# Two-block transformer kernel: the norms between the blocks and the z gate in one block, turned tile by tile

## The chip, the cores and the metric

The kernel runs on one core of a Trainium2 chip. The time is device microseconds of that core; three runs of the kernel before took 3314.9, 3316.67 and 3316.89 us, median 3316.67.

## The reference, cut to what matters

The program computes two layers one after the other. The first has windowed and latent attention and a mixture of 16 experts; the second has a gated delta rule, banded attention and a gated feed-forward layer. All is float32 on 1024 positions of width 1024. The change lies where the first hands over to the second:

```python
def first_block(...):
        ...
        x = x + g_f * ec_moe(h2, w_router[l], w_gate[l], w_up[l], w_down[l])
        ...
    return rmsnorm(x, norm_final)

def second_block(x, norm_mix_w, w_in, ...):
        h = rmsnorm_2(x, norm_mix_w[l])
        proj = h @ w_in[l]
        qa, ka, va, za, ba, aa, qb, kb, vb, ga, gb = jnp.split(proj, IN_SPLITS, axis=-1)
        ...
        oa = (rmsnorm_2(oa, gdn_norm_w[l]) * jax.nn.silu(za)).astype(x.dtype).reshape(b_, t_, VAL_A)
```

So between the experts and the rest stand two norms in a row (weights norm_final and norm_mix), the turn of h so that features lie on partitions (hT), the product z = h @ w_z (1024x512) with Silu and the weight gdn_norm, and the narrow product for ba and aa.

## The kernel before, in words

The 1024 positions are 8 tiles of 128 (NT = 8), the width is 8 slices of 128 (KD = 8). Each stage is a block: five programs, one for each engine, with hand-written semaphores; a block ends when all its engines have arrived. PSUM is one tensor `banks` of 8 banks of 512 floats a partition. A float32 product stands in the trace as two TensorE instructions (passes), so a z tile (8 products of 128x512) is 16 passes; a transpose is one.

`experts` (L1254) runs 16 experts. For each, TensorE does gate_up (products into banks 2 and 3), turn_x (eight transposes of the next expert's rows, evicted in 128x128 pieces by ScalarE at L1352 and VectorE at L1376), down and turn_h. SP loads the weights three experts ahead into three sets of buffers. The last scatter into expert_sums ends the stage.

`between_blocks` (L1402) takes the tiles of x. SP issues the 8 loads of x, then 17 small constants (L1417, norm_mix the eleventh of them), w_z, w_ba, the first two feature weights, and then each x_rows store when its tile is scaled. VectorE's loop does, per step, `first` of tile t (x times norm_final, L1469), `second` of tile t-1 (a reciprocal, x scaled, L1476, the second mean, L1478) and `third` of tile t-2 (a reciprocal and the last scaling into x_weighed, L1486). ScalarE does two squares with sums (L1452, L1457) and two roots (L1435, L1439) per tile. TensorE takes tiles in pairs: it waits for both, turns 16 pieces of 128x128 (L1518) into four banks, and uses the two sets of four banks in turn. ScalarE evicts slices 0 to 3 (L1444) and VectorE slices 4 to 7 (L1493), 256 columns each, times norm_mix, into hT. All wait for all the constants before the first eviction.

`delta_gate_rows` (L1624) is a block of its own. TensorE does eight z tiles (L1647) into banks 0 to 3 in turn; after tile 1 the ba rows (L1653), after tile 3 the picks (L1659), small products that turn them. ScalarE does Silu (L1667) and VectorE the multiplication by gdn_norm (L1685), SP stores each tile. VectorE first makes four sums of quadrants of hT (L1677 to L1682, feat_rows) for the next stage. SP issues w_v at the start.

`delta_features` (L1694) follows with products at L1786, bound by TensorE.

Of the kernel before, what the change touches and what calls it, by code (L numbers as in the profile page):

```python
# [1254 lines left out]
def experts(c, k, d):  # L1255
# [146 lines left out]
def between_blocks(c, k, d, loads, x, xw, junk, stat, hT, w_z, w_ba, ring, ring_in):  # L1402
# [6 lines left out]
    x_out = [c.sem(f"x2_out{i}") for i in range(NT)]  # L1409

    with nc.Block(no_gpsimd_drain=True) as block:
        @block.sync
        def _(sp):
            for t in range(NT):
                sp.dma_start(x[:, t, :], k.y_dram[P * t:P * t + P, :]).then_inc(k.tile_in[t], 16)
            for dst, src in loads:
                sp.dma_start(dst, src).then_inc(k.second_in, 16)  # L1417
            sp.dma_start(w_z[:, :, :], d["w_z"]).then_inc(k.w_z_in, 16)
            sp.dma_start(w_ba[:, :, :], d["w_ba"]).then_inc(k.w_z_in, 16)
            for i in range(2):  # L1420
                sp.dma_start(ring[i][:, :, :], d["w_feat"][i]).then_inc(ring_in[i], 16)
            for t in range(NT):
                sp.wait_ge(scaled, t + 1)
                sp.dma_start(k.x_dram[P * t:P * t + P, :], x[:, t, :]).then_inc(x_out[t], 16)
            for t in range(NT):
                sp.wait_ge(x_out[t], 16)

        def turned_at(g, q):
            return c.ps[:, 4 * BANK * (g % 2) + 2 * P * q:4 * BANK * (g % 2) + 2 * P * q + 2 * P]

        @block.scalar
        def _(act):
# [8 lines left out]
            def turned_out(g):  # L1441
                act.wait_ge(turned, g + 1)
                for q in range(4):
                    last = nc.scalar.activation(hT[:, q, 2 * P * g:2 * P * g + 2 * P], turned_at(g, q), ACT.Identity, scale=k.norm_mix[:, q:q + 1])  # L1444
                last.then_inc(by_act, 1)

            for t in range(NT + 2):
# [12 lines left out]
                if t >= 3 and t % 2 == 1:  # L1460
                    if t == 3:
                        act.wait_ge(k.second_in, 16 * len(loads))
                    turned_out((t - 3) // 2)

        @block.vector
        def _(dve):
# [21 lines left out]
            def turned_out(g):  # L1488
                dve.wait_ge(turned, g + 1)
                if g == 0:  # L1490
                    dve.wait_ge(k.second_in, 16 * len(loads))
                for q in range(4, KD):
                    last = nc.vector.tensor_scalar(hT[:, q, 2 * P * g:2 * P * g + 2 * P], turned_at(g, q), k.norm_mix[:, q:q + 1], None, ALU.mult)  # L1493
# [5 lines left out]
            for t in range(NT + 3):  # L1499
# [6 lines left out]
                if t >= 4 and t % 2 == 0:  # L1506
                    turned_out((t - 4) // 2)

        @block.tensor
        def _(pe):  # L1510
            for g in range(NT // 2):
                pe.wait_ge(normed, 2 * g + 2)
                if g >= 2:
                    pe.wait_ge(by_act, g - 1)
                    pe.wait_ge(by_dve, g - 1)
                for q in range(KD):
                    for j in range(2):
                        last = nc.tensor.transpose(turned_at(g, q)[:, P * j:P * j + P], xw[:, 2 * g + j, P * q:P * q + P], k.ident[:, :])  # L1518
                last.then_inc(turned, 1)


def first_experts(c, k, d):
# [27 lines left out]
    k.norm_rows = k.tmp  # L1550
    experts(c, k, d)
# [70 lines left out]


def delta_gate_rows(c, k, d, hT, w_z, w_ba, ba_rows, z, w_v, T, T3):  # L1624


    nc = c.nc
    rows_summed, ba_made, ba_out, ba_picked = c.sem("z_rows_summed"), c.sem("ba_made"), c.sem("ba_out"), c.sem("ba_picked")
    B11, B12, B21, B22 = (hT[:, 4 * a:4 * a + 4, BANK * b:BANK * b + BANK] for a in range(2) for b in range(2))
    product, copied, weighed, stored = (c.sem(f"z_{s}") for s in ("product", "copied", "weighed", "stored"))  # L1630
    with nc.Block(no_gpsimd_drain=True) as block:
        @block.sync
        def _(sp):
            sp.dma_start(w_v[:, :, :], d["w_vb"]).then_inc(k.w_v_in, 16)
            for t in range(NT):
                sp.wait_ge(weighed, t + 1)
                sp.dma_start(k.z_dram[t], z[:, t]).then_inc(stored, 16)
            sp.wait_ge(stored, 16 * NT)

        @block.tensor  # L1640
        def _(pe):
            pe.wait_ge(k.w_z_in, 32)
            for t in range(NT):
                if t >= 4:
                    pe.wait_ge(copied, t - 3)
                for q in range(KD):
                    last = nc.tensor.matmul(c.bank(t % 4), hT[:, q, P * t:P * t + P], w_z[:, q, :], start=q == 0, stop=q == KD - 1)  # L1647
                last.then_inc(product, 1)
                if t == 1:
                    for half in range(2):  # L1650
                        for q in range(KD):
                            g = 32 * (q % 4)
                            last = nc.tensor.matmul(c.bank(4 + half)[g:g + 32, :], w_ba[:, q, :], hT[:, q, BANK * half:BANK * half + BANK],  # L1653
# [1620 lines left out]
```

## Time and profile before

| | us |
|---|---|
| median of three runs | 3316.67 |
| span of the profiled execution, first to last instruction | 3312.2 |
| what lies around the span (median less span) | 4.5 |
| TensorE busy in the span | 3117.9 |
| between_blocks, first x load to last eviction | 1336.3 to 1379.2 |
| z products, first to last | 1379.57 to 1443.16 |
| next stage's first product | 1447.05 |

TensorE is busy nearly throughout; its busy time counts slow passes too, so the granted clock is read beside it (1.00 is 2.4 GHz, 0.50 is 1.2 GHz; a value between is the mean of a stretch with both). Times in the timelines are us from the start of the span. A row that stands for several instructions gives the time from the start of the first to the end of the last.

### The profile page before, as it was taken

The page shows a single profiled execution, that of the slowest core. Times are in us where ns is not written, and L with a number is a line of the kernel's source. Part 1 is how long each engine was busy: PE and PEld are TensorE (multiplying, and loading weights), DVE is VectorE, ACT ScalarE, POOL GpSimd, SP SyncE. Part 2 cuts the span into 40 slices and gives each one's busy share as a digit, 9 for nine tenths or more (in the row PEclk, how much of TensorE's full clock was granted, in tenths as well). Part 3 has the DMA queues.
Part 4 walks back from the last instruction along what each step waited for, and adds up shares of the span by engine and source line. Part 5 has one row for each costly group of instructions (what it writes and reads, how often), then busy time and mean ns, then how long its engine had stood idle before and what let it go on. Part 6 is the DMA issues. An engine that isn't in the chain of part 4 may idle for free. (4 is left out here: it accounts for less than half of the span.)

```text
span 3312.2 us, 35441 instructions
## 1 busy us (share of the span) xinstructions
PE 3117.9 (94%) x14154; PEld 1647.6 (50%) x14154; DVE 1331.6 (40%) x2223; ACT 780.3 (24%) x1548; POOL 621.2 (19%) x519
## 2 busy tenths in 40 slices
PE   7998989999949999599999988999999999999998
PEld 3457656665424444244456656444444444444443
DVE  2226437673351111524322465314525444544233
ACT  3126534442211111312212036111011211111001
POOL 0005400000000110023022125322203232321323
PEclk9999999999969999699999999999999999999999
DMA  7210000003267885501000130012101111113443
GB/s 287 76 51 29 1 26 1 1 1 155 115 249 295 331 332 174 202 32 38 29 24 27 52 134 2 32 51 95 70 38 51 51 39 39 50 38 141 137 132 130
DMA packets 65826, 311.38 MB, mean 94 GB/s; under 512 B 10240, under 2 KB 11776, under 8 KB 51840
## 3 DMA queue, kind: packets, MB, share of 16 engines
q1 hardware_dynamic: 61056, 292.35, 23.6%
q0 software_dynamic: 4608, 16.78, 2.0%
q8 instruction: 113, 1.85, 0.2%
q14 instruction: 49, 0.40, 0.0%
HBM read 272.39 MB, written 36.70 MB: 93 GB/s over the span
## 5 line engine op out<-in xcount | busy, mean ns | idle before, releaser
L2697 PE MATMUL banks<-hT,ffn_ring 128*128 128x512 f32 x528 | 235.7, 596 | 1.1 <-PEq L2393 1.1
L2857 PE MATMUL banks<-down_ring,down_sums 128*128 128x512 f32 x440 | 189.2, 592 | 0.0
L2697 PEld LDWEIGHTS banks<-hT,ffn_ring 128*128 128x128 f32 x528 | 101.0, 192 | 128.4 <-issue 128.3
L822 PE MATMUL banks<-kT_b,qT_b 96*128 96x512 f32 (+1 forms) x384 | 158.7, 523 | 3.5 <-ACT prob_b L884 2.4
L2697 PE MATMUL banks<-ffn_row_sums,ffn_w_sums 128*128 128x512 f32 x352 | 158.3, 592 | 1.2 <-DVE ffn_row_sums L2737 1.2
L330 PE MATMUL banks<-w_in,hT 128*128 128x512 f32 (+1 forms) x384 | 157.5, 567 | 1.2 <-PEq L157 1.2
L2747 DVE SCALAR_TENSOR_TENSOR ffn_acc<-ffn_u,s_ffn_taps,ffn_acc 128x1023 f32<-128x1023 f32 x88 | 125.0, 1421 | 68.0 <-ACT ffn_acc L2730 66.4
L2857 PEld LDWEIGHTS banks<-down_ring,down_sums 128*128 128x128 f32 x440 | 83.6, 190 | 105.2 <-issue 103.8
L728 POOL TENSOR_TENSOR prob<-prob,softmax_columns 128x640 f32<-128x640 f32 (+1 forms) x64 | 75.4, 1199 | 312.4 <-DVE softmax_columns L686 312.4
L1592 PE MATMUL banks<-hT,side_ring 128*128 128x512 f32 x256 | 127.5, 617 | 1.3 <-PEq L2208 1.3
L2666 POOL TENSOR_TENSOR ffn_w_sums<-ffn_ring 128x512 f32<-128x512 f32 x22 | 35.1, 1596 | 473.8 <-DMA ffn_ring<-in_w_ffn 344.2
L1315 PE MATMUL banks<-expert_wg,expert_xT 128*128 128x512 f32 x256 | 114.5, 601 | 2.4 <-ACT expert_xT L1352 1.7
L2838 POOL TENSOR_TENSOR down_sums<-actT 128x512 f32<-128x512 f32 x55 | 79.4, 1446 | 196.7 <-PE banks L2857 173.0
L1056 PE MATMUL banks<-w_out,OT 128*128 128x512 f32 x256 | 113.3, 602 | 2.0 <-PEq L86 2.0
L1279 POOL DMA_INDIRECT expert_x<-xn_rows,idxT x16 | 15.7, 983 | 530.1 <-POOLq L1018 522.6
L1331 PE MATMUL banks<-expert_wd,expert_hT 128*128 128x512 f32 x256 | 112.6, 593 | 1.2 <-DVE expert_y L1386 1.2
L330 PEld LDWEIGHTS banks<-w_in,hT 128*128 128x128 f32 x384 | 71.8, 190 | 81.8 <-issue 78.5
L1315 PE MATMUL banks<-expert_wu,expert_xT 128*128 128x512 f32 x256 | 112.5, 592 | 0.0
L2490 PE MATMUL banks<-w_out,sigmoids 128*128 128x512 f32 x256 | 111.0, 592 | 0.0
L859 DVE TENSOR_REDUCE softmax_columns_b<-banks 128x1 f32<-128x1280 f32 x64 | 95.4, 1491 | 36.9 <-PE banks L822 36.9
L2697 PEld LDWEIGHTS banks<-ffn_row_sums,ffn_w_sums 128*128 128x128 f32 x352 | 66.8, 190 | 85.7 <-issue 85.7
L884 ACT ACTIVATE prob_b<-banks,softmax_columns_b 128x1280 f32<-128x1280 f32 x64 | 84.9, 1327 | 93.2 <-DVE softmax_columns_b L859 93.2
(509 smaller groups left out, 5379.4 us busy)
## 6 DMA issues: line engine op xcount, KB each, us to landing
down_ring<-in_w_down SPq DMA_DIRECT2D x132, 256.0 KB, 2.9
expert_wg<-in_w_gate SPq DMA_DIRECT2D x16, 2048.0 KB, 15.4
expert_wu<-in_w_up SPq DMA_DIRECT2D x16, 2048.0 KB, 20.8
expert_wd<-in_w_down SPq DMA_DIRECT2D x16, 2048.0 KB, 8.5
ffn_ring<-in_w_ffn SPq DMA_DIRECT2D x22, 1024.0 KB, 4.8
wmod_slab<-in_w_mod SPq DMA_DIRECT2D x6, 2048.0 KB, 7.9
wmod_ring<-in_w_mod SPq DMA_DIRECT2D x4, 2048.0 KB, 10.9
w_out<-in_w_out SPq DMA_DIRECT2D x4, 2048.0 KB, 8.5
```

The source lines that it names most:

```text
L330: last = nc.tensor.matmul(c.ps[:, base + a:base + b], h[:, q, :], k.w_in[i][:, q, 0:b - a], start=q == 0, stop=q == KD - 1)
L822: last = nc.tensor.matmul(scores(u)[:, a:b], heads[u // 2].q[u % 2], heads[u // 2].keys[u % 2][:, a:b], start=True, stop=True, skip_group_ ...
L859: nc.vector.reduce_max(st[:, 0, u % 2:u % 2 + 1], scores(u), AX.X, negate=True).then_inc(negmax, 1)
L884: nc.scalar.activation(prob[:, u % 3, :], scores(u), ACT.Exp, bias=st[:, 0, u % 2:u % 2 + 1], accum_out=st[:, 1, u % 2:u % 2 + 1]).then_in ...
L1056: last = nc.tensor.matmul(c.bank(i % 4), k.OT[:, q, P * t:P * t + P], k.w_out[half][:, q, :], start=q == 0, stop=q == KD - 1)
L1315: last = nc.tensor.matmul(c.bank(b), xT[:, e % 2, q, :], w[e % 3][:, q, :], start=q == 0, stop=q == KD - 1)
L1331: last = nc.tensor.matmul(c.bank(5 + half), hT[:, f, :], wd[e % 3][:, f, BANK * half:BANK * half + BANK], start=f == 0, stop=f == KF - 1)
L1592: last = nc.tensor.matmul(self.c.bank(6 + half), self.ring[:, f % 2, q, :], self.hT[:, q, BANK * half:BANK * half + BANK], start=q == 0, s ...
L2490: last = nc.tensor.matmul(c.bank(i % 4), sig[:, q, P * t:P * t + P], w_o[half][:, q, :], start=q == 0, stop=q == KD - 1)
L2697: last = nc.tensor.matmul(product(f, m), wt[:, q, :], x[:, q, :], start=q == 0 and m != 2, stop=q == 3, skip_group_check=True)
L2747: nc.vector.scalar_tensor_tensor(acc[:, g, j:SEQ], u[:, g, 0:SEQ - j], k.ffn_taps[:, (f * 2 + g) * 4 + 2 - j:(f * 2 + g) * 4 + 3 - j], acc ...
L2857: last = nc.tensor.matmul(c.bank(4 - 4 * (p % 2) + t), stationary[:, P * t:P * t + P], w[s % RING][:, 0, :], start=j == 0, stop=j == N - 1)
```

## The change

between_blocks and delta_gate_rows become one block, `join_blocks`. Each tile is turned alone (8 transposes) into two banks, the tiles using banks 4 and 5 and banks 6 and 7 in turn, and evicted alone in pieces of 128x128. TensorE's order is turn(0), turn(1), gate(0), turn(2), turn(3), gate(1), turn(4), turn(5), gate(2), turn(6), turn(7), gate(3) to gate(7), where gate(t) is the z product of tile t into banks 0 to 3 in turn; the ba rows come after gate(5) (banks 4 and 5), the picks after gate(6). gate(t) waits for both evictions of tile t. ScalarE's Silus and VectorE's sums and multiplications follow their loops over the tiles. The sums now wait for the x_rows stores, since they write where x is stored from. w_z is loaded at the end of the experts' block, into the place that the third set of expert weights leaves; norm_mix is loaded right behind x with a semaphore of its own; w_v is loaded when all tiles are turned.

```diff
@@ experts, sync
+            sp.wait_ge(s["hidden"], NE - 1)
+            sp.dma_start(k.w_z[:, :, :], d["w_z"]).then_inc(k.w_z_in, 16)
@@ join_blocks, sync
             for t in range(NT):
                 sp.dma_start(x[:, t, :], k.y_dram[P * t:P * t + P, :]).then_inc(k.tile_in[t], 16)
+            sp.dma_start(k.norm_mix[:, :], d["norm_mix"]).then_inc(mix_in, 16)
             for dst, src in loads:
                 sp.dma_start(dst, src).then_inc(k.second_in, 16)
-            sp.dma_start(w_z[:, :, :], d["w_z"]).then_inc(k.w_z_in, 16)
-            sp.dma_start(w_ba[:, :, :], d["w_ba"]).then_inc(k.w_z_in, 16)
+            sp.dma_start(w_ba[:, :, :], d["w_ba"]).then_inc(k.second_in, 16)
...
+            sp.wait_ge(turned, NT)
+            sp.dma_start(w_v[:, :, :], d["w_vb"]).then_inc(k.w_v_in, 16)
+            for t in range(NT):
+                sp.wait_ge(gated, t + 1)
+                sp.dma_start(k.z_dram[t], z[:, t]).then_inc(stored, 16)
...
-        def turned_at(g, q):
-            return c.ps[:, 4 * BANK * (g % 2) + 2 * P * q:4 * BANK * (g % 2) + 2 * P * q + 2 * P]
+        def turned_at(t, q):
+            return c.ps[:, (4 + 2 * (t % 2)) * BANK + P * q:(4 + 2 * (t % 2)) * BANK + P * q + P]
@@ scalar
-            for t in range(NT + 2):
+            for t in range(NT + 3):
...
-                if t >= 3 and t % 2 == 1:
+                if t >= 3:
                     if t == 3:
-                        act.wait_ge(k.second_in, 16 * len(loads))
-                    turned_out((t - 3) // 2)
+                        act.wait_ge(mix_in, 16)
+                    turned_out(t - 3)
+            for t in range(NT):
+                act.wait_ge(product, t + 1)
+                nc.scalar.activation(z[:, t], c.bank(t % 4).rearrange("p (h n) -> p h n", h=GH), ACT.Silu).then_inc(copied, 1)
@@ vector
-                if t >= 4 and t % 2 == 0:
-                    turned_out((t - 4) // 2)
+                if t >= 3:
+                    turned_out(t - 3)
+            dve.wait_ge(by_act, NT)
+            dve.wait_ge(by_dve, NT)
+            dve.wait_ge(weighed_sq, NT)
+            for t in range(NT):
+                dve.wait_ge(x_out[t], 16)
+            nc.vector.tensor_tensor(T[:, 0, :, :], B12, B11, ALU.subtract).then_inc(rows_summed, 1)
...
+            dve.wait_ge(k.second_in, 16 * (len(loads) + 1))
+            for t in range(NT):
+                dve.wait_ge(copied, t + 1)
+                nc.vector.tensor_tensor(z[:, t], z[:, t], k.gdn_norm[:, :].unsqueeze(1).to_broadcast([P, GH, P]), ALU.mult).then_inc(gated, 1)
@@ tensor
-            for g in range(NT // 2):
-                pe.wait_ge(normed, 2 * g + 2)
-                if g >= 2:
-                    pe.wait_ge(by_act, g - 1)
-                    pe.wait_ge(by_dve, g - 1)
+            def turn(t):
+                pe.wait_ge(normed, t + 1)
+                if t >= 2:
+                    pe.wait_ge(by_act, t - 1)
+                    pe.wait_ge(by_dve, t - 1)
                 for q in range(KD):
-                    for j in range(2):
-                        last = nc.tensor.transpose(turned_at(g, q)[:, P * j:P * j + P], xw[:, 2 * g + j, P * q:P * q + P], k.ident[:, :])
+                    last = nc.tensor.transpose(turned_at(t, q), xw[:, t, P * q:P * q + P], k.ident[:, :])
                 last.then_inc(turned, 1)
+
+            def gate(t):
+                if t == 0:
+                    pe.wait_ge(k.w_z_in, 16)
+                pe.wait_ge(by_act, t + 1)
+                pe.wait_ge(by_dve, t + 1)
+                if t >= 4:
+                    pe.wait_ge(copied, t - 3)
+                for q in range(KD):
+                    last = nc.tensor.matmul(c.bank(t % 4), hT[:, q, P * t:P * t + P], w_z[:, q, :], start=q == 0, stop=q == KD - 1)
+                last.then_inc(product, 1)
+
+            turn(0)
+            turn(1)
+            for t in range(NT):
+                gate(t)
+                if t < 3:
+                    turn(2 * t + 2)
+                    turn(2 * t + 3)
+                if t == 5:
...
+                if t == 6:
...
```

## Rows read from the trace of the kernel before

**Rows 1.** The page, first part: busy time, share, instructions of each engine.
```profile
PE 3117.9 (94%) x14154; PEld 1647.6 (50%) x14154; DVE 1331.6 (40%) x2223; ACT 780.3 (24%) x1548; POOL 621.2 (19%) x519
```

**Rows 2.** One stretch: PE, PEld, DVE, ACT, POOL busy; granted clock, DMA share, GB/s.
```profile
1350.00:1379.50 29.50, 14.08 (x64) 12.48 (x64) 21.69 (x47) 17.87 (x44) 0.00 (x0) 0.56 0.79 295
```

**Rows 3.** Waits, 1336 to 1380: who waited for whom, us in total, times, longest.
```profile
PE banks L1518 <- DVE x_weighed L1486: 36.5, 4, 23.1
```

**Rows 4.** Timeline of TensorE: start, us, instructions, idle before and releaser.
```profile
1350.04 3.67 PE L1518 MATMUL banks<-ident,x_weighed 128*128 128x128 f32 x16 [23.12 <-DVE x_weighed L1486]
...
1367.91 3.67 PE L1518 MATMUL banks<-ident,x_weighed 128*128 128x128 f32 x16 [5.23 <-DVE x_weighed L1486]
...
1379.57 16.84 PE L1647 MATMUL banks<-w_z,hT 128*128 128x512 f32 x32 [2.09 <-PEq L1411]
...
1415.45 27.71 PE L1647 MATMUL banks<-w_z,hT 128*128 128x512 f32 x64
1447.05 5.24 PE L1786 MATMUL banks<-hT,feat_ring 128*128 128x512 f32 x8 [3.89 <-PEq L1631]
```

**Rows 5.** Timeline of VectorE and ScalarE, 1345 to 1390.
```profile
1345.92 1.04 ACT L1452 ACTIVATE junk<-x 128x1024 f32<-128x1024 f32 x1
...
1348.51 1.04 ACT L1452 ACTIVATE junk<-x 128x1024 f32<-128x1024 f32 x1
...
1349.23 0.75 DVE L1486 TENSOR_SCALAR x_weighed<-x,join_stat 128x1024 f32<-128x1024 f32 x1
...
1350.92 0.28 ACT L1439 ACTIVATE join_stat<-join_stat,eps 128x1 f32<-128x1 f32 x1
...
1352.22 0.76 DVE L1486 TENSOR_SCALAR x_weighed<-x,join_stat 128x1024 f32<-128x1024 f32 x1
1353.75 1.66 DVE L1493 TENSOR_SCALAR hT<-banks,s_norm_mix 128x256 f32<-128x256 f32 x4 [0.78 <-PE banks L1518]
...
1358.20 0.75 DVE L1486 TENSOR_SCALAR x_weighed<-x,join_stat 128x1024 f32<-128x1024 f32 x1
...
1386.30 2.28 DVE L1682 TENSOR_TENSOR feat_rows<-feat_rows,hT 128x2048 f32<-128x2048 f32 x1
...
1389.58 0.60 ACT L1667 ACTIVATE z_rows<-banks 128x512 f32<-128x512 f32 x1 [8.78 <-PE banks L1647]
```

**Rows 6.** Timeline in the experts: a turn and its evictions; gate_up(14).
```profile
1267.36 1.04 PE L1304 MATMUL banks<-ident,expert_x 128*128 128x128 f32 x8
...
1268.23 7.03 PE L1331 MATMUL banks<-expert_wd,expert_hT 128*128 128x512 f32 x16
1268.43 1.50 ACT L1352 ACTIVATE expert_xT<-banks,mod,scale_f 128x128 f32<-128x128 f32 x4 [0.28 <-PE banks L1304]
...
1268.79 1.36 DVE L1376 TENSOR_SCALAR expert_xT<-banks,scale_f,mod 128x128 f32<-128x128 f32 x4
...
1282.40 7.03 PE L1315 MATMUL banks<-expert_wu,expert_xT 128*128 128x512 f32 x16
```

**Rows 7.** Stretches of 1 us: busy us, granted clock, DMA share; TensorE, then all engines.
```profile
1371.00:1372.00 1.00, 0.59 (x3) 0.65 1.01 410
...
1385.00:1386.00 1.00, 1.00 (x4) 0.82 1.11 475
...
1450.00:1451.00 1.00, 1.00 (x3) 0.43 (x3) 0.00 (x0) 0.00 (x0) 1.00 (x2) 0.90 0.00 0
```

**Rows 8.** DMA issues, 1325 to 1460: count, KB each, median us to landing.
```profile
x_rows<-x SPq DMA_DIRECT2D x8, 512.0 KB, 13.9
w_z<-in_w_z SPq DMA_DIRECT2D x1, 2048.0 KB, 7.6
...
s_tri<-in_tri SPq DMA_DIRECT2D x1, 64.0 KB, 8.6
```

**Rows 9.** A stretch in the experts: TensorE busy, granted clock, DMA share, GB/s.
```profile
1292.00:1293.00 1.00, 1.00 (x4) 1.00 0.00 0
```

More of the change, by code:

```diff
@@ L1399, in _, with join_blocks @@
             result(NE - 1)
-def between_blocks(c, k, d, loads, x, xw, junk, stat, hT, w_z, w_ba, ring, ring_in):
+def join_blocks(c, k, d, loads, x, xw, junk, stat, hT, w_z, w_ba, ring, ring_in, ba_rows, z, w_v, T, T3):
     nc = c.nc
@@ L1408, in between_blocks @@
                                      "normed", "turned", "by_act", "by_dve"))
-    x_out = [c.sem(f"x2_out{i}") for i in range(NT)]
+    x_out, mix_in = [c.sem(f"x2_out{i}") for i in range(NT)], c.sem("norm_mix_in")
+    rows_summed, ba_made, ba_out, ba_picked = c.sem("z_rows_summed"), c.sem("ba_made"), c.sem("ba_out"), c.sem("ba_picked")
+    product, copied, gated, stored = (c.sem(f"z_{s}") for s in ("product", "copied", "weighed", "stored"))
+    B11, B12, B21, B22 = (hT[:, 4 * a:4 * a + 4, BANK * b:BANK * b + BANK] for a in range(2) for b in range(2))
     with nc.Block(no_gpsimd_drain=True) as block:
@@ L1486, in third, with turned_out @@
                 nc.vector.tensor_scalar(xw[:, t, :], x[:, t, :], stat[:, 6, t:t + 1], None, ALU.mult).then_inc(normed, 1)
[L1488 to L1491, printed above, removed]
+            def turned_out(t):
+                dve.wait_ge(turned, t + 1)
+                if t == 0:
+                    dve.wait_ge(mix_in, 16)
                 for q in range(4, KD):
[L1493 removed]
+                    last = nc.vector.tensor_scalar(hT[:, q, P * t:P * t + P], turned_at(t, q), k.norm_mix[:, q:q + 1], None, ALU.mult)
                 last.then_inc(by_dve, 1)
@@ new lines, in _ @@
+            turn(0)
[5 more added lines that the diff above has]
+                    turn(2 * t + 3)
+                if t == 5:
+                    pe.wait_ge(by_act, NT)
+                    pe.wait_ge(by_dve, NT)
+                    pe.wait_ge(k.second_in, 16 * (len(loads) + 1))
+                    for half in range(2):
+                        for q in range(KD):
+                            g = 32 * (q % 4)
+                            last = nc.tensor.matmul(c.bank(4 + half)[g:g + 32, :], w_ba[:, q, :], hT[:, q, BANK * half:BANK * half + BANK],
+                                                    start=q < 4, stop=q >= 4, skip_group_check=True)
+                    last.then_inc(ba_made, 1)
+                if t == 6:
+                    pe.wait_ge(ba_out, 1)
+                    for i in range(NT):
+                        last = nc.tensor.matmul(c.bank(6)[:, 8 * i:8 * i + 8], ba_rows[:, i // 4, P * (i % 4):P * (i % 4) + P], k.pick8[:, :], start=True,
+                                                stop=True, skip_group_check=True)
+                    last.then_inc(ba_picked, 1)
@@ L1550, in first_experts @@
     k.norm_rows = k.tmp
+    k.w_z, k.w_z_in = c.area("w_z", F + 5680, KD, 512), c.kept_sem("w_z_in")
     experts(c, k, d)
```

87 lines of the change are left out of this document (21 added, 66 removed).

## The prediction, made before the changed kernel was run

> **What bounds the kernel now.** I read the page first, then the busy time by stretch around the join, then the waits there, then the timelines of TensorE, VectorE and ScalarE. The page's first part says that TensorE is busy for 94% of the span [rows 1]; a change that takes idle or slow TensorE time away therefore shows in the end nearly one for one, and one that only relieves another engine does not. The join is one of the few places where TensorE isn't full: from 1350 to 1379.5 us it is busy for 14.1 of 29.5 us, and that at a mean granted clock of 0.56 [rows 2]. The waits say for whom: four waits of 36.5 us in all on VectorE's line 1486, the last scaling of a tile [rows 3]. So the stretch before the z products is set by the VectorE chain (weigh, scale, scale again, per tile), which turns and evictions interrupt. Behind it come the z products, 1379.57 to 1443.16 us, in which TensorE is full [rows 4]: four tiles take 27.71 us, so 6.9 us each at the full clock, and the first takes 10.0 us (1379.57 to 1389.58, where its Silu starts [rows 5]), because the clock stood at 0.50 until about 1385.4 [rows 7]. The products need hT tile by tile, and before they get nothing until all of it is made. That is what can be overlapped: TensorE work of 64 us beside VectorE and ScalarE work that runs anyway.
>
> **Until the first product.** Nothing of the chain of the first three tiles changes: the same eight loads of x stand first in SP's queue, and tile 1 is scaled by 1349.98 (1349.23 + 0.75), tile 2 by 1352.98 [rows 5], a tile interval of 3.0 us. turn(0) now needs tile 0 alone and runs at about 1347, turn(1) at 1350.04, each 1.84 us (half of 3.67 for sixteen transposes at the low clock [rows 4]). ScalarE comes to eviction 0 after the second root of tile 2, at 1351.20 [rows 5]; four pieces of 128x128 took it 1.50 us in the experts [rows 6], so it ends at 1352.7. VectorE does its four in 1.36 us [rows 6] from 1350.0, done 1351.4. The later one decides: gate(0) starts at **1352.75**.
>
> Two new waits stand ahead of it. norm_mix is now issued behind the x loads, in the slot where s_tri went; s_tri landed 8.6 us after its issue at about 1340.2 [rows 8], so about 1348.8, 1.2 us before VectorE's eviction and 2.4 us before ScalarE's. I take nothing; if it came up to 3 us late, VectorE (third, first and second of the later tiles queue behind it) and gate(0) would lose up to 1.5 us. w_z took 7.6 us to land [rows 8]. It is issued after gate_up(14), whose last pass ends at 1289.4 [rows 6], and the DMA engines have nothing to do then (share 0.00 [rows 9]); it is in by about 1297, 55 us early. Cost nothing: SP has nothing else queued behind that wait, and the buffer that it fills (experts' third pair of weights) has had its last reader. In the join the 2 MB are gone from the queue, so the ring loads and x_rows stores come some us sooner; nobody on the path waits for those.
>
> **The first product.** From 1352.75 TensorE has work without a stop, so the clock must rise, and the question is when. The rows give three rises: 3.8 us after a run of transposes began (1367.91 to about 1371.7), 5.8 us after the z products began and 3.15 us after the feature products began (1447.05 to about 1450.2), all read from a mean between 0.5 and 1 [rows 4, 7]. A 128x512 pass takes 0.855 us at the low clock and 0.43 at the high one. A rise after 3.15 us makes 3.7 slow passes and 12.3 fast ones, 8.5 us; after 5.8 us, the measured 10.0. If turn(0) and turn(1) already count and the clock rises at once, 7.0. I take **9.2**, the middle of the two measured ones, since the gap of almost 1 us ahead of gate(0) resembles neither.
>
> The Trainium skill ("TensorE: Matmul & The Clock Gate", Part 4) says that transposes don't count as activity for the gate. The rows speak against it: the clock rose during transposes alone [rows 4, 7]. By that rule the first product would take the full 9.8 to 10.0 us and the time would be 3295.5, inside the forecast.
>
> **The turns between products.** turn(2) to turn(7) now stand between gate(0) and gate(3). In the experts a turn of eight at the full clock moves the next instruction by 0.87 us (1267.36 to 1268.23 [rows 6]); six make **5.2 us**. They used to run before, in time that TensorE idled.
>
> **One bubble.** turn(2) waits behind gate(0), and VectorE and ScalarE stand at eviction 2 until it is done. After that VectorE does eviction 2, one tile, eviction 3, one tile, before tile 5 is scaled: 2 x 1.36 + 2 x 3.0 = 8.7 us, or 9.8 if both tile intervals take the 3.54 us seen behind an eviction (1355.41 to 1358.95 [rows 5]). TensorE meanwhile does turn(3), gate(1), turn(4): 0.87 + 6.9 + 0.87 = 8.6 us, and then needs tile 5. Bubble 0.1 to 1.2 us, I take **0.5**. Tiles 6 and 7 are scaled before gate(2) ends, so gates 2 and 3 follow without one. ScalarE's share per tile, 2.6 us (1345.92 to 1348.51 [rows 5]) and an eviction of 1.5, is shorter than VectorE's 4.4 and sets nothing.
>
> Against splitting the evictions stands a rule of the Trainium skill ("VectorE: DVE Perf Modes", the section on the TRN2 errata): a large tile pays an instruction's fixed latency once, small ones each time. The rows agree: four pieces of 128x256 took 1.66 us and four of 128x128 still 1.36 [rows 5, 6], so eight evictions cost VectorE 10.9 us where four cost 6.6. By the rows that 4.3 us lies beside TensorE's products and is worth the bubble alone; were it all on the path, the time would be 3298.6.
>
> **The rest.** From the first tile's Silu (1389.58) to the last pass (1443.16) are **53.6 us**: seven tiles, the ba rows and the picks. They are unchanged; ba is now after gate(5) and the picks after gate(6), where the evictions of all tiles have long been out of banks 4 to 7. ScalarE does its Silus only behind its last eviction, about 1384, plus the table load; gate(4) starts about 1388.5 and needs the first of them, which is there by 1386. VectorE's four sums of 2.28 us each [rows 5] now come behind its last eviction, and behind x_out. The last x_rows store is issued at about 1374, with the median landing of 13.9 us [rows 8] it is in by 1388. The sums end by about 1398, and the z multiplications, 0.7 us each, catch up by 1402. Cover: until about 1418. The tail stays: last pass, Silu, multiplication, store, and the next stage's first product 3.9 us after the last pass [rows 4], again at the low clock. The block boundary that goes away (about 0.4 us) is in these times, since I count from start to end.
>
> **The sum.** 1352.75 + 9.2 + 5.2 + 0.5 + 53.6 = 1421.25 against 1443.16: **21.9 us** less. Everything behind is TensorE-bound and relative to this point, so the span goes from 3312.2 to 3290.3. The median of the runs stands 4.5 us above the span; 3316.67 - 21.9 = **3294.8**. The known bounds: first product -2.2/+0.8, bubble -0.4/+0.7, norm_mix 0/+1.5, the clock's rise behind the new tail -0/+1.4 (it rose after 3.15 us there, near the fast end), some us for what can't be costed: 3292 to 3299.
>
> **The rivals.** *A, engines on each other's heels (0.15).* VectorE and ScalarE meet at three handshakes per tile and at evictions, and TensorE's order is fixed: turn(4) and turn(5) both stand ahead of gate(2). If the tile intervals after stalls stretch, or if evictions run slower beside products, each of the pairs 2-3, 4-5 and 6-7 leaves 1.5 to 4 us. For it: 3.54 instead of 3.0 behind an eviction [rows 5]. Against: the experts' evictions ran beside products at 1.36 and 1.50 us [rows 6]. It gives 3299 to 3309, say 3303. *B, the clock (0.04, the slower side).* The gate stays at the low level while products and turns alternate with waits, as in the join now, where it showed 0.50 nearly throughout [rows 2]. Until gate(3) is done that costs gate(0) 4.5, three gates 6.85 each and six turns 0.97 each: 30.9 us, and the time would be 3325.7. It decides from about the end of gate(2): if the clock is still low there, the gain is gone. Against it: each of the three runs of work above saw the clock rise within 5.8 us [rows 4, 7], and gate(0) alone is longer. The Trainium skill, same page, names such a case ("A second HAM failure mode"), micro-idles between groups of products that make the clock oscillate; the trace before doesn't show it. *C, given back (0.05).* Something behind the stage has an absolute time, a load or a store that was covered by the 22 us. I find none: the ring loads and w_v land 50 us before use. It would give 3310 to 3316, about no change. *D, more (0.06).* The clock is up at gate(0) and the feature stage starts warmer: 3290 to 3292.
>
> **How the numbers follow.** Forecast 3294.8 with 0.70; A 0.15, B 0.04, C 0.05, D 0.06. The range 3291 to 3302 holds the forecast's, most of D, and the nearer half of A: about 0.83. About 0.2% (6.6 us, so the line lies at 3310) is what a measurement of this kernel can tell from no change: faster 0.92, same 0.04, slower 0.04.
>
> **What would show it.** Right: the first z product at 1352 to 1353.5; it ends by 1363; the eight turns in pairs between gates; no wait of TensorE over 1.2 us behind it, and granted clock 1.00 from about 1358; VectorE's four sums between 1384 and 1398; last z pass near 1421; next stage 3.9 us later. Wrong: a first product later than 1355 (norm_mix or w_z late, read it from its wait), waits of TensorE on line 1486 or on the evictions over 3 us in sum (A), a clock row of 0.50 behind 1362 (B), or a stage behind the join that is longer than before by more than 2 us (C).

## The result, and the profile after

The changed kernel takes 3295.25 us (median of four runs, 3294.2 to 3296.76) beside 3315.78 us for the kernel before in the same comparison: ratio 0.9938, 95% interval 0.9924 to 0.9952, so 20.5 us less. The forecast was 3294.8 from a base of 3316.67. The span fell from 3312.2 to 3292.1, by 20.1 us, where the sum had said 21.9. These near hits hide two errors of opposite sign, which the traces show: the join became 23.5 us shorter where the sum had 21.9, and 3.3 us of that were given back far behind it.

The page of the changed kernel: TensorE's busy time is what it was (3117.9 [rows 1]); the share rises because the span shrinks.

```profile
span 3292.1 us, 35481 instructions
PE 3118.0 (95%) x14154; PEld 1646.2 (50%) x14154; DVE 1335.6 (41%) x2239; ACT 782.6 (24%) x1564; POOL 623.1 (19%) x519
```

TensorE's timeline of the changed kernel, to be laid beside [rows 4]: L1552 turns, L1563 z products, L1580 ba rows, L1586 picks, L1792 feature products.

```profile
1347.13 1.97 PE L1552 MATMUL banks<-ident,x_weighed 128*128 128x128 f32 x8 [20.16 <-DVE x_weighed L1506]
1350.12 1.97 PE L1552 MATMUL banks<-ident,x_weighed 128*128 128x128 f32 x8 [1.02 <-DVE x_weighed L1506]
1352.39 8.42 PE L1563 MATMUL banks<-w_z,hT 128*128 128x512 f32 x16 [0.31 <-issue]
1360.65 1.91 PE L1552 MATMUL banks<-ident,x_weighed 128*128 128x128 f32 x16
1362.40 7.03 PE L1563 MATMUL banks<-w_z,hT 128*128 128x512 f32 x16
1369.27 1.91 PE L1552 MATMUL banks<-ident,x_weighed 128*128 128x128 f32 x16
...
1379.63 20.77 PE L1563 MATMUL banks<-w_z,hT 128*128 128x512 f32 x48
...
1412.57 7.11 PE L1563 MATMUL banks<-w_z,hT 128*128 128x512 f32 x16
1423.64 5.20 PE L1792 MATMUL banks<-hT,feat_ring 128*128 128x512 f32 x8 [3.96 <-PEq L1416]
```

From 1352.39 to 1419.68 TensorE has no idle time at all: the rows behind the first z product carry no bracket. The four waits of 36.5 us on the tile scaling [rows 3] have become two, of which only the first is long and was there before (20.2 us until tile 0 is scaled).

VectorE and ScalarE in the changed kernel, against [rows 5]: the first two evictions, VectorE's waits for turn(2) and turn(4), its last sum and ScalarE's last Silu.

```profile
1350.31 1.13 DVE L1513 TENSOR_SCALAR hT<-banks,s_norm_mix 128x128 f32<-128x128 f32 x4 [0.25 <-DMA s_norm_mix<-in_norm_mix]
...
1361.73 1.13 DVE L1513 TENSOR_SCALAR hT<-banks,s_norm_mix 128x128 f32<-128x128 f32 x4 [3.29 <-PE banks L1552]
...
1370.34 1.13 DVE L1513 TENSOR_SCALAR hT<-banks,s_norm_mix 128x128 f32<-128x128 f32 x4 [0.48 <-PE banks L1552]
...
1387.95 2.28 DVE L1538 TENSOR_TENSOR feat_rows<-feat_rows,hT 128x2048 f32<-128x2048 f32 x1
```
```profile
1351.18 1.12 ACT L1455 ACTIVATE hT<-banks,s_norm_mix 128x128 f32<-128x128 f32 x4
...
1419.72 0.60 ACT L1477 ACTIVATE z_rows<-banks 128x512 f32<-128x512 f32 x1 [6.75 <-PE banks L1563]
```

In stretches of 1 us (TensorE busy, granted clock, DMA share) the clock comes up at 1355, 2.6 us into the first product. Far behind, at 2068, it falls at a place where it had stayed at 1.00 in the kernel before.

```profile
1354.00:1355.00 1.00, 1.00 (x2) 0.50 1.04 434
1355.00:1356.00 1.00, 1.00 (x4) 0.98 0.98 401
...
2068.00:2069.00 1.00, 0.15 (x1) 0.72 0.00 0
2069.00:2070.00 1.00, 1.00 (x2) 0.50 0.00 0
```

Where the 3.3 us went: I laid both timelines of TensorE over each other. The lead of the changed kernel is 23.4 us at the first feature product and 23.3 at the start of the banded attention (1965.74 and 1942.41), 21.6 at the gate products (2083.67 and 2062.04), 20.15 from their third group on (2093.99 and 2073.84), and 20.1 at the end. Both losses are the same instructions at the low clock. The kernel before, start of the attention and second group of the gate products:

```profile
1969.73 1.13 PE L636 MATMUL banks<-band_qkT 64*128 64x256 f32 x8
1971.67 0.66 PE L620 MATMUL banks<-ident,band_prob 128*128 128x128 f32 x4 [0.81 <-POOL band_prob L728]
...
2090.48 3.67 PE L2474 MATMUL banks<-gate_rows,gate_sums 128*128 128x512 f32 x8 [3.14 <-DVE gate_rows L2535]
```

The changed kernel, the same two:

```profile
1946.65 2.08 PE L636 MATMUL banks<-band_qkT 64*128 64x256 f32 x8
1948.66 1.11 PE L620 MATMUL banks<-ident,band_prob 128*128 128x128 f32 x4
...
2068.85 5.16 PE L2480 MATMUL banks<-gate_rows,gate_sums 128*128 128x512 f32 x8 [3.14 <-DVE gate_rows L2541]
```

TensorE's busy time at the low clock grew by 6.3 us at the attention (3.3 to 9.6) and by 3.0 at the gate products (none before); everywhere else behind the join it is the same to 0.3 us. By an estimate, work at half the clock takes twice as long, so these 9.3 us should cost 4.7; 3.3 were lost. A part of the rest shows in the rows: at the attention TensorE waited 0.81 us for POOL before, and slowed down it doesn't.

### The profile page after: what moved, and what is told of

Its sections match the earlier page's. It is cut to its first block and busy times, and to the rows that moved or that the text cites. A ratio compares the mean times of both kernels' runs of the same rounds, so it can differ in the third digit from the quotient of the medians.

```text
span 3292.1 us, 35481 instructions
## 1 busy us (share of the span) xinstructions
PE 3118.0 (95%) x14154; PEld 1646.2 (50%) x14154; DVE 1335.6 (41%) x2239; ACT 782.6 (24%) x1564; POOL 623.1 (19%) x519
## 5 line engine op out<-in xcount | busy, mean ns | idle before, releaser
L2672 POOL TENSOR_TENSOR ffn_w_sums<-ffn_ring 128x512 f32<-128x512 f32 x22 | 32.8, 1491 | 472.3 <-DMA ffn_ring<-in_w_ffn 342.7
```

## The experiments

The start of the join stands elsewhere in each profile (its first reciprocal at 1341.7 to 1345.8 us, with the same code ahead of it). So times in the join are given behind that first reciprocal on VectorE, which is at 1342.42 in the kernel before and at 1342.49 in the changed one. "Tail stage" below is the time from the first feature product to TensorE's last product, the same code in all kernels. Its low-clock time is my sum over stretches of 1 us: TensorE's busy time, times the share of the stretch at 0.50.

**The changed kernel again.** No edit.

> The changed kernel again, unedited, to see what of the trace repeats. Up to the first feature product everything should stand within 0.3 us of the first profile (first z product 1352.4, last z pass 1419.7, feature products 1423.6), 23.4 us ahead of the kernel before. Behind it the first profile gave 3.3 us back in two places, both stretches at the low clock (1.8 us at the start of the banded attention, 1.5 us at the second group of the gate products). If that is chance (where the clock's change falls), the two differences vary from run to run between 0 and about 2 us each and the span lies between 3289 and 3294; if it is a cost of the change, both repeat to 0.2 us and the span is 3292 again. Time against before: 20 to 23 us less.

Ratio 0.9939 (0.9925 to 0.9952), median 3295.69: 18.8 us less than before, a little under the 20 to 23 expected. The span is 3294.2, 2.1 us longer than in the first profile, and all of that lies ahead of the join, whose first reciprocal stands 2.3 us later (1344.76). The join repeats: last z pass 77.1 us behind the reciprocal (77.2 the first time). The two losses repeat too, which I had half expected to be chance:

```profile
1948.81 2.08 PE L636 MATMUL banks<-band_qkT 64*128 64x256 f32 x8
```
```profile
2070.96 5.15 PE L2480 MATMUL banks<-gate_rows,gate_sums 128*128 128x512 f32 x8 [3.14 <-DVE gate_rows L2541]
```

**The kernel before again.** No edit.

> The kernel before again, unedited, for its low-clock stretches. The changed kernel lost 1.7 us at the start of the banded attention and 1.5 us at the second group of the gate products in two profiles, against one profile of before. If that is chance of one profile of before, this one differs from the first by up to 2 us in at least one of the two places; if it is bound to the kernels, it repeats the first: band to gate products 117.9 us, gate products to the seventh group 20.6 us.

One time, 3315.21 us. The same two places, both at the full clock again:

```profile
1970.83 1.13 PE L636 MATMUL banks<-band_qkT 64*128 64x256 f32 x8
...
2091.59 3.67 PE L2474 MATMUL banks<-gate_rows,gate_sums 128*128 128x512 f32 x8 [3.14 <-DVE gate_rows L2535]
```

Band to gate products 117.94 us, gate products to the seventh group 20.62, both as in the first profile of before. So the 3.3 us are not one lucky profile of before; they come back with the kernel.

**All turns first.**

```diff
-            turn(0)
-            turn(1)
             for t in range(NT):
+                turn(t)
+            for t in range(NT):
                 gate(t)
-                if t < 3:
-                    turn(2 * t + 2)
-                    turn(2 * t + 3)
```

> One block, tile by tile, w_z early, all as in the changed kernel, but TensorE does all eight turns before the first z product. Theory (the gain is the z products beside the norms): the eighth eviction ends near 1374.3, first z product there, at the low clock for 3 to 6 us, last z pass near 1437, span 15 to 19 us longer than the changed kernel's, so still some 5 us shorter than before. Rival (the gain is in the parts: one block boundary fewer, finer tiles, w_z early): within 3 us of the changed kernel.

Ratio to before 0.9979 (0.997 to 0.9988), median 3306.24. TensorE again waits for VectorE between turns, four times about 2 us:

```profile
1362.02 1.97 PE L1552 MATMUL banks<-ident,x_weighed 128*128 128x128 f32 x8 [2.05 <-DVE x_weighed L1506]
...
1372.58 42.56 PE L1563 MATMUL banks<-w_z,hT 128*128 128x512 f32 x96
```

The last z pass stands at 92.4 behind the reciprocal, against 77.2 with the products between the turns and 100.7 in the kernel before. So 15.2 of the join's 23.5 us are the overlap, and 8.3 are the rest: the products start 6.6 us earlier (finer tiles and the missing boundary, which no run separates), and the first of them is 1.7 us shorter, because the clock rises after 2.4 us of z products here and 5.8 in the kernel before. The theory holds in kind, and its sizes were too high: the last z pass stands 2 us earlier than I expected, 1.3 of it because gate(0) follows turn(7) at once and doesn't wait for the eighth eviction, and the tail stage is 1.7 us shorter than in the changed kernel. By the medians the kernel is 10.6 us slower than the changed one (3295.69 in this comparison), with runs from 3303.4 to 3312.4, where 15 to 19 were expected.

**w_z in the join's queue.** The two lines leave the experts' block, and the same load stands ahead of w_ba.

```diff
-            sp.wait_ge(s["hidden"], NE - 1)
-            sp.dma_start(k.w_z[:, :, :], d["w_z"]).then_inc(k.w_z_in, 16)
...
+            sp.dma_start(w_z[:, :, :], d["w_z"]).then_inc(k.w_z_in, 16)
             sp.dma_start(w_ba[:, :, :], d["w_ba"]).then_inc(k.second_in, 16)
```

> Only the place of the w_z load is undone: it stands in the join's queue behind the constants, issued at about 1350.8. Theory: gate(0) waits for it and starts at about 1358.4 in place of 1352.4, all behind it shifts by 5 to 7 us and the span with it (3297 to 3299). Rival (the early load is worth nothing, since the products have slack): the last z pass stays at 1419.7.

Ratio 0.9951 (0.9938 to 0.9965), median 3299.06.

```profile
1360.29 9.99 PE L1562 MATMUL banks<-w_z,hT 128*128 128x512 f32 x16 [7.03 <-DMA w_z<-in_w_z]
```

gate(0) waits 7.0 us for the load and starts 6.8 us later than in the changed kernel (16.7 against 9.9 behind the reciprocal); the clock rises 5.8 us into the first product instead of 2.6, so that product takes 9.99 us. The last z pass is 8.4 us later, 1.4 more than the 5 to 7 expected. In the join the early load is a third of the gain. In the time it is 3.4 us, since the tail stage is 4.4 us shorter here than in the changed kernel (1854.5 against 1858.9).

**Turning in pairs.** turned_at, both evictions and the waits count pairs of 256 columns in banks 4 to 7; TensorE's order is turn(0), gate(0), turn(1), gate(1), turn(2), gate(2), turn(3), gate(3) and on.

```diff
-                pe.wait_ge(normed, t + 1)
+                pe.wait_ge(normed, 2 * g + 2)
...
-                    last = nc.tensor.transpose(turned_at(t, q), xw[:, t, P * q:P * q + P], k.ident[:, :])
+                    for j in range(2):
+                        last = nc.tensor.transpose(turned_at(g, q)[:, P * j:P * j + P], xw[:, 2 * g + j, P * q:P * q + P], k.ident[:, :])
```

> One block, w_z early, z products between the turns, but tiles are turned and evicted in pairs of 256 columns in one set of four banks, as before the change. Theory: the pair is turned from 1350.1 to 1353.8 at the low clock and evicted by 1355.4, so gate(0) starts 3 us later than in the changed kernel, and nothing else changes: last z pass 1422 to 1424, span 2 to 5 us longer than the changed kernel's. Rival (the finer tiles carry the change): over 8 us longer.

Ratio 0.9945 (0.9931 to 0.9959), median 3296.83.

```profile
1353.29 3.67 PE L1553 MATMUL banks<-ident,x_weighed 128*128 128x128 f32 x16 [23.26 <-DVE x_weighed L1506]
```
```profile
1358.81 10.17 PE L1564 MATMUL banks<-w_z,hT 128*128 128x512 f32 x16 [1.84 <-DVE hT L1513]
```

gate(0) starts 3.25 us later, as forecast, and its product is 1.75 us slower (10.17 against 8.42) because the clock rose 6.2 us into it: 5.0 us in the join, so the last z pass misses its forecast by 1.7. The single set of four banks shows no wait. Tile by tile is a fifth of the gain in the join. The three shares, 15.2, 8.4 and 5.0 us, add up to more than the 23.5, so they are not parts side by side: each is what is missing when its piece alone is taken out. The medians stand only 1.1 to 1.6 us apart. In the profile the tail stage is 1 us shorter here; but the profiled run was the slowest of the five (3301.46, median 3296.83), so how the others made up the rest isn't shown.

**Evicting twice.** VectorE writes each piece first to a spare place, then to hT.

```diff
+                for q in range(4, KD):
+                    nc.vector.tensor_scalar(again[:, t, q - 4, :], turned_at(t, q), k.norm_mix[:, q:q + 1], None, ALU.mult)
                 for q in range(4, KD):
```

> The changed kernel in which VectorE evicts each of its pieces twice (the first time to a spare place), 1.04 us more per tile, 8.3 in all. Theory: TensorE sets the pace and VectorE is close behind it at one place: between the end of turn(2) and the scaling of tile 5 it needs 8.1 us against TensorE's 8.6, so 2.1 us more open a bubble of about 1.6 ahead of turn(5), and gate(0) starts up to 0.3 us later; the other six evictions stay hidden. Last z pass 1.5 to 2.5 us later. Rival: evictions are on the path tile by tile, 8 us later; or all hidden, 0.

Median 3296.41, ratio 0.9945 (0.9931 to 0.9958). The one bubble opens where it was forecast, ahead of turn(5), and nowhere else:

```profile
1351.89 9.89 PE L1566 MATMUL banks<-w_z,hT 128*128 128x512 f32 x16 [0.63 <-DVE hT L1516]
...
1372.95 1.09 PE L1555 MATMUL banks<-ident,x_weighed 128*128 128x128 f32 x8 [1.68 <-DVE x_weighed L1507]
```

8.3 us more of VectorE work cost 1.7 us of bubble and 0.3 at gate(0). The last z pass is 3.7 us later, more than the 1.5 to 2.5 expected; the missing 1.5 is once more the first product (9.89 against 8.42 us). The median is only some 1 us above the changed kernel's, with runs from 3294.0 to 3299.9, so this verdict rests on the timeline, not on the time. The profiled run was one of the two slowest (3299.94).

**Spare products at the head.** Twelve products of identity and w_z where TensorE waits, into banks 0 to 3.

```diff
+            pe.wait_ge(k.w_z_in, 16)
+            spare(9)
             turn(0)
+            spare(2)
             turn(1)
+            spare(1)
```

> The changed kernel with twelve spare products (identity times w_z into banks that are written over later) where TensorE waits in the join: nine ahead of turn(0), two between the turns, one ahead of gate(0). Theory: what the first product costs over 7.0 us is the low clock alone, and its start is set by ScalarE's eviction. So the first product still starts 9.9 us behind the first reciprocal of the join, takes 7.0 in place of 8.4 us, and the last z pass comes 1.4 us earlier. Rival: the first product is slow because hT's first slices have only just been written, or the spare products delay the turns: no gain, or a loss of up to 2 us.

```profile
1336.55 10.38 PE L1568 MATMUL banks<-w_z,ident 128*128 128x512 f32 x18 [9.34 <-PEq L86]
...
1352.53 7.10 PE L1563 MATMUL banks<-w_z,hT 128*128 128x512 f32 x16 [0.33 <-issue]
```

The clock rises within the nine spare products, at 1341.4, and stays up to the end of the join. gate(0) starts where it did (9.9 behind the reciprocal), takes 7.10 us, and the last z pass is 1.3 us earlier: that theory holds. But the time fell by 7 us, not 1.4: median 3287.89, ratio 0.992 (0.9906 to 0.9933). By the profile the other 5.7 us are in the tail stage (1853.2 against 1858.9), which was not touched.

**The narrow work at the end.** ba rows of the second half and all picks behind gate(7), ScalarE's copies split in two halves.

```diff
                 if t == 5:
...
+                    ba(0)
+            ba(1)
+            pick(0)
+            pick(1)
```

> The changed kernel with the narrow work at the end: the ba rows of the first half stay after gate(5), those of the second half and both picks come after gate(7), so they lie beside the Silu, the multiplication and the store of the last z tile. Theory: the 3.96 us between the last pass and the first feature product are that chain and not the block boundary; with 3.5 us of TensorE work beside it, the feature products start 3.4 us earlier, after an idle gap of 0.5 to 1 us, and the clock doesn't fall, so their first group takes 3.6 in place of 5.2 us: 5 us less in all, span near 3287 at the same start of the join. Rival: the gap is the block boundary itself (barrier, branches): it stays near 4 us behind the picks, and nothing is won.

> The kernel with the narrow work at the end, unedited, as the version to keep: time against before 0.990 to 0.991, and the stretch from the first feature product to the last product repeats its 1851.6 us to 0.2 us, as the two profiles of the changed kernel and the two of before did.

Ratio 0.9904 (0.9889 to 0.992) and in the second comparison 0.9909 (0.9894 to 0.9924), medians 3283.22 and 3284.08: the fastest version, some 32 us less than before and 12 less than the changed kernel.

```profile
1417.57 1.92 PE L1560 MATMUL banks<-hT,w_ba 128*32 128x512 f32 x16
1419.42 1.95 PE L1567 MATMUL banks<-s_pick,ba_rows 128*128 128x8 f32 x16
1421.96 3.67 PE L1800 MATMUL banks<-hT,feat_ring 128*128 128x512 f32 x8 [0.58 <-PEq L1416]
```

The gap of 3.96 us is 0.58 now, so it was the chain of Silu, multiplication and store, not the block boundary. The chain itself is no shorter: the feature products still start 4.3 us behind the last z pass (1417.64), and what is won is that 3.8 us of narrow work, which used to stand ahead of it, lie in that time. The feature products start 3.3 us earlier and their first group takes 3.67 us instead of 5.20, which makes 4.8 of the 5 us expected. Another 5.8 are again in the tail stage, behind that group (7.3 us shorter in all). By the profiles that is 10.6 us, by the medians 11 to 12.

**Spare products in the tail.** The changed kernel, nothing moved, four products behind gate(7) in TensorE's idle time.

```diff
+            for i in range(4):
+                nc.tensor.matmul(c.bank(4 + i % 2), k.ident[:, :], w_z[:, i, :], start=True, stop=True)
```

> The changed kernel with four spare products behind gate(7), 3.4 us at the full clock, in the 3.96 us in which TensorE waits for the last store; nothing else moves. Two theories of the 12 us that the kernel with the narrow work at the end was shorter than the changed one. Clock: 3.2 us of it come from the earlier start of the feature products, the rest from the clock, 1.5 us at their first group and the rest from stretches far behind that it visits at the low clock or not, depending on what went before. Then this kernel's feature products start no earlier (behind the join's first reciprocal 81.1 us), their first group takes 3.6 in place of 5.2 us, and the stage behind differs from the changed kernel's by more than that 1.5 us. Work: the gain comes with the moved work; then this one gains 1.5 us at most and the rest repeats (feature products to the end 1857.3 us).

```profile
1422.76 3.60 PE L1590 MATMUL banks<-w_z,ident 128*128 128x512 f32 x8
1426.88 3.67 PE L1794 MATMUL banks<-hT,feat_ring 128*128 128x512 f32 x8 [0.52 <-PEq L1416]
```

Median 3290.83, ratio 0.9927 (0.9913 to 0.994). The feature products start at 81.1 behind the reciprocal, as in the changed kernel, and yet the tail stage is 5.7 us shorter (1853.1 against 1858.9), of which 1.5 us are its first group. Four products whose results nobody reads are worth 4.4 to 4.9 us by the medians (runs from 3288.7 to 3293.6, beside 3291.4 to 3296.8 of the changed kernel): the clock theory stands, the work theory falls.

**One spare product in front of the features.** The kernel with the narrow work at the end, plus one product of 0.86 us.

```diff
             pick(1)
+            nc.tensor.matmul(c.bank(0), k.ident[:, :], w_z[:, 0, :], start=True, stop=True)
```

> The kernel with the narrow work at the end, plus one spare product (0.86 us) behind the picks, so that the feature products start 0.3 to 0.9 us later and all behind it is the same code. If the low-clock stretches behind depend on fine timing alone, their sum changes from 20.5 us by several us (up to 39) and the time by -1 to +8 us; if they belong to the tail's structure, they stay and the time grows by 0.3 to 0.9 us.

```profile
1418.94 1.10 PE L1597 MATMUL banks<-w_z,ident 128*128 128x512 f32 x2
1420.46 3.67 PE L1801 MATMUL banks<-hT,feat_ring 128*128 128x512 f32 x8 [0.41 <-PEq L1416]
```

The features start 0.95 us later (78.8 against 77.85), the tail stage grows by 2.8 us, its low-clock time from 20.6 to 29.3 us. Median 3286.64, about 3 us above the kernel without that product. The code behind the join is the same; a start 0.95 us later and one product ahead of it made the difference, and which of the two isn't separated.

**Both edits.**

> Both edits, spare products ahead of the first z product and the narrow work at the end. If the two theories hold they add up: 1.4 + 5.0 = 6.4 us less than the changed kernel, about 27 us (0.8%) less than before. If the two share a cause, less than their sum.

Median 3285.5, ratio 0.9913 (0.99 to 0.9927): not better than the narrow work alone. It is 29.8 us less than before, more than the 27 expected, and yet far from the sum of what the two edits bring alone by the medians (some 7 and 12 us less than the changed kernel, both together 10). The join is the shortest of all (last z pass at 72.4), but the feature products behind the same idle gap of 0.58 us now meet the low clock, and their first group takes 5.37 us instead of 3.67.

```profile
1420.59 5.37 PE L1808 MATMUL banks<-hT,feat_ring 128*128 128x512 f32 x8 [0.58 <-PEq L1416]
```
```profile
1420.00:1421.00 1.00, 0.42 (x2) 1.00 0.00 0
1421.00:1422.00 1.00, 1.00 (x2) 0.50 0.00 0
```

**The tail stage in all profiles.** Identical code, identical work:

| kernel | features start behind the reciprocal, us | tail stage, us | of it busy at the low clock, us |
|---|---|---|---|
| before, two profiles | 104.6, 104.7 | 1855.6, 1855.6 | 29.4, 29.6 |
| changed, two profiles | 81.15, 81.06 | 1858.9, 1858.8 | 39.0, 38.8 |
| all turns first | 96.4 | 1857.2 | 35.8 |
| w_z in the join | 89.5 | 1854.5 | 29.3 |
| pairs | 86.15 | 1857.9 | 32.8 |
| evicting twice | 84.85 | 1862.0 | 45.0 |
| spare products at the head | 79.8 | 1853.2 | 24.0 |
| narrow work at the end, two profiles | 77.81, 77.85 | 1851.6, 1851.6 | 20.5, 20.7 |
| the same and one spare product | 78.8 | 1854.4 | 29.3 |
| spare products in the tail | 81.1 | 1853.1 | 25.3 |
| both edits | 76.7 | 1853.4 | 23.1 |

The length follows the low-clock time, and both repeat to 0.2 us in the three kernels that have two profiles. It does so in the main only: by an estimate, taking half of the low-clock time off each length leaves 1839.3 to 1841.9 us, so 2.6 of the 10 us of spread are something else, such as waits that a slower TensorE fills. The low stretches are not strewn at random either. In every profile of the table those behind the first group lie at the same few waits of TensorE, nearly all of 2.3 to 5.3 us, about 174, 231, 416, 518, 645, 1050 and 1597 us behind the first feature product (pairs has one more, at 483); what differs is which of these bring the clock down, and for how long. The kernel before slows at all of them but 645, the narrow work at the end only at 174, 518, 1050 and 1597.

What decides between them is not settled. It isn't the start of the stage, since the changed kernel and the one with spare products in the tail start it at the same time; nor the clock at its first group, which is the full one both with the narrow work at the end and with one spare product more (20.5 and 29.3 us). Nor is it shown how far it is bound to the kernel. The timed runs of the kernel before spread over 7 us (3309.92 to 3317.29 in 15 runs), those of the evicting-twice kernel over 6, where those of the narrow work spread over 3. In the three kernels with two profiles the spans differ by 1.1, 2.1 and 1.8 us, and all of it lies ahead of the join. But the profile of evicting twice is of a run 3.5 us above the median of its kernel, although its join started as early as any (1341.66), so its other runs probably had less than these 45.0 us.

## Why the prediction came out right, step by step

**Start of the first product**, forecast 1352.75, measured 1352.39. The deciding engine was right, ScalarE; its eviction took 1.12 us instead of 1.50. The experts' rows [rows 6] were too dear; those evictions add a shift beside the scale, which is the difference between the two lines and the likely reason, though no run changes it alone. norm_mix landed 10.0 us after its issue at 1340.22, not 8.6, so at 1350.2: VectorE waited 0.25 us for it, and ScalarE, which decides, did not.

**The first product**, forecast 9.2 from measured bounds of 8.5 to 10.0, measured 8.26 (1352.39 to 1360.65). The clock rose 2.6 us into it, a little before any rise in [rows 4, 7]. That transposes don't bring the clock up, as the Trainium skill has it ("TensorE: Matmul & The Clock Gate", Part 4), would have made it 9.8 to 10.0; it did not come out so here, but with w_z in the join and with pairs the first product did take 10.0 and 10.2 us. No run had transposes alone taken away. What speaks against the rule is one rise in the kernel before, and the prediction read it a little wrong: the transposes ended at 1371.58, and the clock rose 0.1 us behind them (0.65 in the stretch from 1371 is 0.70 us at the low clock, and TensorE was busy for 0.59 of it [rows 7]), after TensorE had done nothing but transposes since 1350. The two runs of transposes before that one, at 1350.04 and 1359.01, brought no rise (0.50 from 1350 to 1367.9).

**The turns**, forecast 5.2, measured 5.24 (three times 1.75). **The bubble**, forecast 0.5, measured none: the term was sized with evictions of 1.36 us, and at 1.13 VectorE needs 8.1 us against TensorE's 8.6. Its place was right, as evicting twice showed. **Splitting** the evictions cost VectorE 8 x 1.13 = 9.0 us against 6.6, 2.4 us in place of the 4.3 forecast, and all of it was hidden. The rule against splitting that the prediction takes from the Trainium skill ("VectorE: DVE Perf Modes", the section on the TRN2 errata) is told there of instructions that read SBUF; these evictions read PSUM, so only the rows carry the figure.

**The rest**, forecast 53.6, measured 53.8, and **the tail** 3.9, measured 3.96. **Covers**: w_z was in 7.7 us after 1289.5; the sums ended at 1390.2 and the z multiplications caught up by 1392.7; x_rows never showed as a wait (median landing 8.8 us, with 2 MB less in the queue).

**"Everything behind is TensorE-bound and relative to this point"** is the step that failed. It was true of every wait and every transfer, and not of the clock: 9.6 us more of the tail stage ran at the low clock, and 3.3 us of the join's 23.5 were lost. The sum had 1.4 us for the clock at the head of that stage and nothing for the clock behind it, although the trace of before has 29.4 us of such work there. The prediction's own sign for rival C, a stage behind the join longer by more than 2 us, came: it was 3.3. Rival C had the sign of a give-back, but not its size (it said 3310 to 3316) nor its mechanism, loads and stores, none of which moved. Rival A did not occur: from 1352.39 to the end of the join TensorE waited for nobody. Its range was mis-added too: three pairs at 1.5 to 4 us each end at 3307, not 3309. Rival B did not occur in the join (0.98 and more from 1355 on), but it names the engine property that mattered, elsewhere. Both ideas of rival D came about by edits of their own: the clock up at gate(0) with spare products at the head, a warmer start of the features with the narrow work at the end or four spare products in the tail. VectorE's sums began at 1381.2, earlier than the 1384 to 1398 given.

**The base**: I took the 4.5 us between the span of the profile and the median as what lies around the span. In the later profiles with their own times it is 2.7 us (3294.77 and 3292.1) and 1.8 (3315.21 and 3313.4). With these, the first profile of before belongs to a run of 3314 to 3315 us, a short one; the comparison of the medians, 20.5 us, is the better measure of the change, and it is 1.4 less than the 21.9 forecast. That 3294.8 agrees with the profiled run's 3294.77 to the digit is luck: the span came out 1.8 us above its forecast, and the 4.5 us were 1.8 too many.

## What to carry to other kernels

Where the busiest engine waits for a chain that works tile by tile, and its next stage needs only one tile at a time, put that stage between the tiles and load its weights a stage ahead; the overlap gave two thirds of the join's gain here, and without the early load a third of it would have been lost. Look at what stands at the end of such a stage: if the last eviction and store leave the busiest engine idle, move small work there that doesn't depend on them. And when a kernel's time moves by a few us, sum the time at the low clock before looking for a cause: a change at one place moved stretches 500 us behind it.

## What the runs showed of the hardware that was not expected

- The same code, behind joins of different length, spent 20.5 to 45.0 us of TensorE's busy time at 1.2 GHz, and took 1851.6 to 1862.0 us: a spread of 10 us, larger than many edits. The low stretches lie at the same few waits each time; which of them, and how long, differs.
- Spare products that nobody reads gained time: twelve at the head some 7 us, four in the tail 4.4 to 4.9 us, of which only 1.3 and 1.5 lie where they stand.
- The clock fell 0.4 us behind an idle gap of only 0.58 us in one kernel (both edits) and not in another with the same join tail (narrow work at the end); ahead of the gap both had done 3.8 us of narrow work (ba rows and picks).
- Four 128x128 evictions with a scale alone took 1.12 us on ScalarE and 1.13 on VectorE in the join; with scale and shift, in the experts, 1.50 and 1.36.
